# Prompt attention moved block by block into the page stream of a one-core decoder step, and the hand-over of two accumulator banks ahead of the keys-values stage moved up

## What is computed

```python
def diff_attn_prompt(q, k, v, lam):          # query blocks of 128, causal, 4 blocks
        s = jnp.einsum('bqhmd,bkhmd->bhmqk', qi, k) * ATTN_SCALE
        s = jnp.where(kpos[None, :] <= qpos[:, None], s, -jnp.inf)
        p = jax.nn.softmax(s, axis=-1)
        w = p[:, :, 0] - lam * p[:, :, 1]
        return jnp.einsum('bhqk,bkhd->bqhd', w, v)
def diff_attn_sample(q, k_past, v_past, k_new, v_new, lam):   # 8 sequences, 16 pages of 128 past tokens each
    s_past = ...; s_new = ... (causal among the 8 new tokens)
    p = jax.nn.softmax(jnp.concatenate([s_past, s_new], axis=-1), axis=-1)
    w = p[:, :, 0] - lam * p[:, :, 1]
    return einsum(w[..., :P], v_past) + einsum(w[..., P:], v_new)
```

## Time and profile before

| | us |
|---|---|
| median of three runs (lowest, highest) | 2148.5 (2145.39, 2149.3) |
| the profiled execution, its own time | 2154.17 |
| its span, first to last instruction | 2152.3 |
| TensorE busy | 1875.1 (87%) |
| VectorE busy | 838.2 (39%) |
| ScalarE busy | 735.3 (34%) |
| GpSimd busy | 155.8 (7%) |
| moved by DMA | 301.07 MB, mean 140 GB/s |

### The profile page before, as it was taken

The page is one execution under the profiler, slowest core; times in us unless marked ns, Lnnn a source line. Parts: engine busy times, 40 slices in busy tenths (PEclk is TensorE's granted clock), DMA queues, the critical chain, the costliest instruction groups (busy, mean ns, idle before and its releaser), DMA issues.

```text
span 2152.3 us, 43567 instructions
## 1 busy us (share of the span) xinstructions
PE 1875.1 (87%) x17223; PEld 1662.3 (77%) x17223; DVE 838.2 (39%) x1423; ACT 735.3 (34%) x1111; POOL 155.8 (7%) x305
## 2 busy tenths in 40 slices
PE   4997889799999996998757798888866899999998
PEld 2583689799999996998623576767636899999997
DVE  6558223423323333127788422222226433233222
ACT  2423333433333223225433454434312343333222
POOL 2010012100000121001011100000003300000000
PEclk7578999899999998999867899999867899999999
DMA  8748642122222322221200499989880122222222
GB/s 258 253 163 269 220 120 78 53 81 81 81 84 64 87 80 71 60 78 40 95 33 0 141 348 366 380 339 370 328 264 27 52 79 78 88 82 72 81 80 71
DMA packets 245007, 301.07 MB, mean 140 GB/s; under 512 B 10188, under 2 KB 195472, under 8 KB 244816
## 3 DMA queue, kind: packets, MB, share of 16 engines
q1 hardware_dynamic: 241752, 290.22, 40.5%
q10 hardware_dynamic: 2432, 8.16, 1.1%
q0 software_dynamic: 704, 0.95, 0.2%
HBM read 291.92 MB, written 7.37 MB: 139 GB/s over the span
## 4 chain that ended last, share of the span: by engine, by line
PE 68%; DVE 9%; DMA 8%; issue 5%; SPq 5%; ACT 3%; POOL 1%; DVEq 0%; POOLq 0%; ACTq 0%
PE ps L578 53%; PE ps L501 4%; DMA kpg<-in_cache_k 4%; DVE t L1813 2%; SPq L452 2%; PE ps L528 2%; SPq L459 2%; DMA raw<-in_w_ada_mix 1%; DMA vpg<-in_cache_v 1%; PE ps L717 1%; PE ps L952 1%; PE ps L856 1%; DMA raw<-in_w_ada_ffn 1%; DVE l L1893 1%; PE ps L908 1%
## 5 line engine op out<-in xcount | busy, mean ns | idle before, releaser
L578 PE MATMUL ps<-hr,ws 128*128 128x288 f32 x5760 | 783.1, 298 | 48.7 <-ACT rstd L1084 16.2
L578 PEld LDWEIGHTS ps<-hr,ws 128*128 128x128 f32 x5760 | 778.2, 191 | 52.8 <-issue 44.0
L1765 DVE TENSOR_TENSOR ws<-raw,ws 128x1024 fp32r<-128x1024 f32 x200 | 234.9, 1176 | 710.4 <-ACT ws L1210 710.4
L1210 ACT ACTIVATE ws<-raw 128x1024 fp32r<-128x1024 f32 x200 | 201.2, 1008 | 700.5 <-PE ps L578 643.5
L578 PE MATMUL ps<-gr,ws 128*128 128x288 f32 x2112 | 279.4, 294 | 0.0
L578 PEld LDWEIGHTS ps<-gr,ws 128*128 128x128 f32 x2112 | 279.1, 188 | 0.0
L1378 ACT ACTIVATE kTs<-ps 128x512 f32<-128x512 f32 x256 | 139.0, 597 | 177.3 <-PE ps L501 176.7
L501 PE MATMUL ps<-ident,kpg 128*128 128x128 f32 x1024 | 142.8, 285 | 33.1 <-DMA kpg<-in_cache_k 31.6
L501 PEld LDWEIGHTS ps<-ident,kpg 128*128 128x128 f32 x1024 | 115.6, 145 | 60.9 <-ACT kTs L1378 30.4
L528 PE MATMUL ps<-raw,cond 128*32 128x256 f32 x896 | 88.3, 509 | 44.5 <-DMA raw<-in_w_ada_mix 32.6
L578 PE MATMUL ps<-hg,ws 128*128 128x288 f32 x768 | 106.0, 301 | 8.9 <-DVE ws L1765 8.9
(11 more groups left out here) (315 smaller groups left out, 1663.0 us busy)
## 6 DMA issues: line engine op xcount, KB each, us to landing
kpg<-in_cache_k SPq DMA_DIRECT2D x128, 512.0 KB, 5.9
vpg<-in_cache_v SPq DMA_DIRECT2D x128, 512.0 KB, 6.0
raw<-in_ffn_w SPq DMA_DIRECT2D x88, 512.0 KB, 3.7
raw<-in_w_ada_mix SPq DMA_DIRECT2D x48, 512.0 KB, 5.3
raw<-in_w_ada_ffn SPq DMA_DIRECT2D x48, 512.0 KB, 4.7
raw<-in_ffn_w SPq DMA_DIRECT2D x48, 384.0 KB, 3.4
raw<-in_w_ada_kv SPq DMA_DIRECT2D x16, 512.0 KB, 5.4
raw<-in_ssm_w_glu SPq DMA_DIRECT2D x16, 512.0 KB, 4.1
```

The lines of the kernel that those rows point to most:

```text
L578: return mm(ps[:, 4 * s + 2 * tile + h, 0:HALF], ws[:, (u * S + j) % 2, w, k, :], src[:, k0 + k, v, h * HALF:(h + 1) * HALF], start=(k0 + ...
L1210: A(ws[:, w, 0, 0:nk, :].rearrange("p k n -> p (k n)"), raw[:, slot, 0:nk, :].rearrange("p k n -> p (k n)"), ACT.Copy).then_inc(slab_high, 1)
L1765: TT(f(ws[:, w, 1, 0:nk, :]), f(raw[:, slot, 0:nk, :]), f(ws[:, w, 0, 0:nk, :]).bitcast(F32), ALU.subtract).then_inc(raw_done[slot], 1)
```

## The change

Prompt attention has no stage of its own. Turns 2 to 9 of the stream hold the eight heads, one block to each quarter of a turn (block n = 4 x (turn - 2) + quarter). On TensorE the scores of block n come after page 1 of the first quarter and after page 0 of the others; the transposes of block n - 1 come ahead of the values of page 0 of each quarter; the previous head's values come after page 0 of a turn. ScalarE does the block's exps after the quarter's last page, and the head's output after page 1 (behind the sequence's exp); VectorE does `block_turned(n - 1)` and `block_max(n)` ahead of a quarter's copy of turned weights and `block_weights(n)` behind it. The last block and head follow turn 9.

Blocks have one set of buffers now: banks 2 and 3 for scores, bank 2 again for transposes, bank 3 for the head's values; key pages are turned in banks 0 and 1 only, new scores and outputs use the free half of bank 6. `vtok` lies in `raw`, so SyncE waits for the last head's values ahead of the `wo` weights. New values come ahead of new scores at a turn's end. The loops over turns are written out. GpSimd's copies of heads go; VectorE waits for `tri` and for the tokens' writes ahead of the stream.

Ahead of `kv` ScalarE signals `free[1]` right after `root(2)`, by a tiny copy; the copy to `rstd` stays where it was and has a signal of its own, `rstd_kept`, for which `apply("q")` waits on VectorE.

```diff
-    vtok = share("vtok", [P, QB, H, DV], 118 * KB)
-    e01 = share("e01", [P, 2, 2, SEQ], 134 * KB)
+    vtok = raw
+    e01 = share("e01", [P, 2, SEQ], 106 * KB)
...
@@ SyncE @@
                 for b in range(DB, DB + LAG):
                     loads(b, keys=False)
+                sp.wait_ge(pv_full, H)
                 slabs("wo", one)
@@ TensorE @@
-            def block_scores(h, hp, i):
+            def block_scores(n):
+                h, i = n // QB, n % QB
                 w = (i + 1) * P
-                if i == 0:
-                    pe.wait_ge(head_in, h + 1)
-                pe.wait_ge(e_done, h * QB + (i + 1))
+                if n:
+                    pe.wait_ge(wp_copied, n)
+                if i == 0 and h:
+                    pe.wait_ge(head_out, h)
...
-            def block_weights(h, i):
-                pe.wait_ge(w_done, h * QB + (i + 1))
-                pe.wait_ge(wp_copied, h * QB + (i + 1))
+            def block_weights(n):
+                i = n % QB
+                pe.wait_ge(w_done, n + 1)
...
-            def head_values(h, hp):
-                pe.wait_ge(wp_copied, h * QB + (QB + 2))
-                pe.wait_ge(head_out, h + 1)
+            def head_values(h):
+                pe.wait_ge(wp_copied, (h + 1) * QB)
+                if h:
+                    pe.wait_ge(head_out, h)
...
-                    bank = ((par * PAGES + u) * 2 + half) % 3
-                    if not isinstance(at, int) or at > 2:
-                        pe.wait_ge(kt_ready, at - 2)
+                    if at > 1:
+                        pe.wait_ge(kt_ready, at - 1)
...
                     if keys and u < PAGES - 1:
                         turn_page(b, par, u + 1)
+                    n = n0 + u // 4
+                    if u % 4 == 0 and n > 0:
+                        block_weights(n - 1)
                     if vals:
                         values(b, u)
                     if keys:
                         scores(b, par, u)
+                    if vals and u == 0 and n:
+                        head_values(n // QB - 1)
+                    if vals and u % 4 == (u < 2):
+                        block_scores(n)
                     if vals and u % 4 == 2:
                         turn_weights(b, par, u // 4 + 1)
                 if vals:
                     pe.wait_ge(vn_full, 16 * (b - LAG + 1))
                     pe.wait_ge(wt_copied, (b - LAG + 1) * 5 + 1)
+                    new_values(b)
                 if keys:
                     new_scores(b, par)
                 if vals:
-                    new_values(b)
                     outputs(b)
...
+            for b in range(DB + LAG):
+                sequence(b)
+            block_weights(H * QB - 1)
+            head_values(H - 1)
@@ ScalarE @@
             root(2)
+            norm_read(2)
             apply("kv")
-            norm_read(2)
+            A(halves(rstd[:, :]), ps[:, 6:8, 0:HALF], ACT.Copy).then_inc(rstd_kept, 1)
             dense("kv")
...
                 for u in range(PAGES):
+                    if b < DB:
+                        page(b, b, u)
+                    if 0 < b <= DB and u == 1:
+                        weights(b, b)
+                    n = n0 + u // 4
+                    if n > 0 and u == 1:
+                        head_output(n // QB - 1)
+                    if n >= 0 and u % 4 == 3:
+                        block_exp(n)
@@ VectorE @@
                 if vals:
                     weights(b, 0)
-                if soft:
+                if 0 < b <= DB:
                     normalize(b, par)
                 for q in range(4):
+                    n = (b - LAG) * QB + q
+                    if n > 0:
+                        block_turned(n - 1)
+                    if n >= 0:
+                        block_max(n)
                     if vals:
                         weights(b, q + 1)
+                    if n >= 0:
+                        block_weights(n)
                     if keys:
                         scores(b, par, q)
```

More of the change, by code:

```diff
@@ L871, in _ @@
-            for i in range(2):
-                block_scores(0, 0, i)
-            head_pair(0, first=True)
-            with pe.Fori(1, H // 2 - 1) as k:
-                head_pair(k)
-            head_pair(H // 2 - 1, final=True)
-            head_values(H - 1, 1)
-            pe.wait_ge(head_out, H + 1)
             def turn_page(b, par, u):
@@ L888, in turn_page @@
                     at = (b * PAGES + u) * 2 + half
-                    bank = ((par * PAGES + u) * 2 + half) % 3
-                    if not isinstance(at, int) or at > 2:
-                        pe.wait_ge(kt_ready, at - 2)
+                    if at > 1:
+                        pe.wait_ge(kt_ready, at - 1)
                     for h in range(4):
-                        last = turn(ps[:, bank, h * P:(h + 1) * P], kpg[:, slot, 4 * half + h, :])
+                        last = turn(ps[:, half, h * P:(h + 1) * P], kpg[:, slot, 4 * half + h, :])
                     last.then_inc(k_turned, 1)
@@ L1384, in weights, with sequence @@
                 A(q, q, ACT.Exp, bias=mq[:, 1, 0:1], scale=SCALE, accum_out=mq[:, 1, 1:2]).then_inc(e_full, 1)
-            def sequence(b, par, keys=True, soft=True):
+            def sequence(b):
+                n0 = (b - LAG) * QB
                 for u in range(PAGES):
-                    if keys:
-                        page(b, par, u)
-                    if soft and u == 1:
-                        weights(b, par)
-            sequence(0, 0, soft=False)
-            sequence(1, 1)
-            with act.Fori(0, (DB - LAG) // NBUF) as i:
-                for v in range(NBUF):
-                    sequence(i * NBUF + (LAG + v), LAG + v)
-            sequence(DB, DB, keys=False)
+                    if b < DB:
[7 more added lines that the diff above has]
+                        block_exp(n)
+            for b in range(DB + LAG):
+                sequence(b)
+            head_output(H - 1)
+            act.wait_ge(head_out, H)
             act.wait_ge(o_ready, DB + 1)
@@ L1601, in _ @@
                 new_keys(b, b)
+            for s in range(2):
+                pool.wait_ge(tok_put[s], 16 * (6, 4)[s])
             new_values(0)
@@ L2008, in sequence @@
                     outputs(b)
-            sequence(0, 0, vals=False, soft=False)
-            sequence(1, 1, vals=False)
-            with step.loop(0, (DB - LAG) // NBUF, 5 * NBUF) as i:
-                for v in range(NBUF):
-                    sequence(i * NBUF + (LAG + v), LAG + v)
-            sequence(DB, DB, keys=False)
-            sequence(DB + 1, DB + 1, keys=False, soft=False)
+            for b in range(DB + LAG):
+                sequence(b)
+            block_turned(H * QB - 1)
             split(SLABS["wo"] - DENSE0)
```

168 lines of the change are left out of this document (51 added, 117 removed).

## The result

The changed kernel takes 2079.9 us (median of 4 runs, 2070.7 to 2081.5) beside 2148.9 for the kernel before: a ratio of 0.967, interval 0.964 to 0.970. The forecast was 2074, range 2045 to 2105. The profiled execution is one of 2080.7 us with a span of 2078.9, against 2152.3 before.

The account below looks back on a forecast made before the run. It saw an attention stage without transfers, then turns where TensorE waits for pages that SyncE issues late. Terms -120.8 - 12.5 + 38.5 + 10 + 10.6 = -74.2, off the median of 2148.5, gave 2074 us, range 2045 to 2105.

Parts of the forecast that it names:

- Cost 0: Key pages turned in two banks instead of three: no cost, as ScalarE's copies are covered; 7 us if not.
- The stage removed: Prompt attention's own stage goes: first stream scores 122.3 us earlier, +1.5 for a low clock, net -120.8 us.
- The keys-values stage: Its first 96 products start early, beside the making of their input: -12.5 us, between 9 and 13.
- Attention's products: TensorE's prompt-attention work in the six keys-and-values turns: 6.5 us a head, bounds 5.7 and 10.3, +35.5 us in all.
- The stall: At a turn's start the previous head's values wait for VectorE's last weight copy: 3.7 us, five turns, +18.5 us.
- Key-page waits: TensorE's 30.2 us of waits for key pages in six turns: 24 given back as cover, bounds 10 and 30.
- The loop: TensorE's 4.03 us gap where the loop over turns starts over disappears: -4 us.
- The turn's end: New scores now follow new values, so TensorE waits longer for VectorE's output copy: +5 us, 0 to 8.
- Why pages were late: SyncE's loads start 1.23 us apart or more, so 16 key and 16 value pages take some 40 us.
- The last two turns: Turns with values alone: two heads' work partly hidden, with a stall at the first's start, +10 us, bounds 5 and 21.
- The end: Output weights are loaded only after the last head's values, with nothing covering it: +10.6 us, bounds 7 and 13.
- the first rival: Transfers and SyncE keep the turns' pace, so attention only fills waits: 2045 to 2055 us, chance 0.13.

Follow-up runs that it names:

- before_early_bank: Kernel before with only the early signal of free[1] right after the root, the rstd copy with its own signal: 2139.3 us, ratio 0.994.
- before_again: Kernel before, unchanged, run as a kernel of its own: 2151.5 us, ratio 0.9997.
- exp_table: Changed kernel with a tiny exp on ScalarE ahead of the stream, so the exp table is loaded there: 2076.1 us, ratio 0.963.
- all_four: Changed kernel with the edits of copy_first, exp_table, bank7 and wo_early together: 2043.5 us, ratio 0.949.
- best: weights_last, exp_table and wo_early in one kernel: 2039.5 us, ratio 0.948.
- copy_first: Changed kernel with VectorE's copy of the last block's turned weights put ahead of the weight row's scaling at a turn's start: 2050.8 us, ratio 0.953.
- bank7: Changed kernel with new scores in the free part of bank 7 and again ahead of new values: 2078.3 us, ratio 0.967.
- weights_last: copy_first with VectorE's operations on the weights of a turn's last block put behind new scores, bias and output copy: 2043.8 us, ratio 0.951.
- no_attention: Changed kernel with the prompt attention's blocks and heads left out of the stream: 2018.0 us, ratio 0.937.
- before_no_loop: Kernel before with only TensorE's loop over the six turns written out: 2141.2 us, ratio 0.994.
- fixed_pages: no_attention with page addresses computed from SyncE's loop counter instead of read from the page table: 2012.4 us, ratio 0.935.
- wo_early: Changed kernel with the last head's values copied by GpSimd, so output weights load one head earlier, and ScalarE's splits ahead: 2068.7 us, ratio 0.962.

## Why the prediction was right, step by step

The forecast was 6 us too low. The differences in the table, without the 6.0 us ahead of the change, come to -67.5, and the medians differ by 69.0; the forecast was -74.2. The step that the forecast had wrong is what the change costs the stream beside attention: "Cost 0" for two key banks, and no term for the rest. It measured 8 us in the six turns and 4.6 on average in the two before them, and which part of the change it is stays open. Other terms were off both ways, and their sum came near by luck in part.

**The stage removed** was right. GpSimd's memset is followed by the first scores 2.55 us later, as before:

```profile
1066.99 0.10 POOL L1526 MEMSET mark<- 128x1 f32 x1
...
1069.54 1.04 PE L887 MATMUL ps<-kTs,qn 128*32 128x128 f32 x16 [3.10 <-POOL kn L1542]
```

Of the -124.1, 1.9 belong to the early bank (before_early_bank has them too), which leaves -122.2 for -122.3; the +1.5 of a low clock lies in the two turns behind. Without the 6.0 us ahead of the change the first scores would have come at 1075.5, for 1078.

**The keys-values stage** was right, -13.0 for -12.5, with those 1.9 beside: 14.8 by itself in before_early_bank.

**Two turns with keys alone** are where this shows most: "Cost 0 by that cover" for two key banks, and a low clock of +1.5 at most. They cost +7.5. Busy time of the first, after:

```profile
1069.54:1098.20 28.66, 25.14 (x368) 19.21 (x369) 4.13 (x6) 15.32 (x28) 2.50 (x11) 0.94 0.72 243
```

and in before_again:

```profile
1206.60:1233.10 26.50, 23.61 (x368) 18.11 (x369) 4.13 (x6) 15.38 (x29) 2.48 (x11) 1.00 0.86 293
```

TensorE comes out of a 3.1 us wait for GpSimd's new keys and is granted 0.94 in place of 1.00; it is busy 1.5 us longer in this turn, and as much in the next. The rest are waits, over both turns 3.2 for ScalarE's page copies (0.8 before) and 3.5 for pages (1.4). Of the copies' waits 1.4 go with the table load, now in the second turn (exp_table). The 7.5 is not the typical size: the four profiles of kernels with the old stream have 53.0 to 55.2 us for these two turns, the seven with the changed kernel's two turns (exp_table, all_four and best aside) 56.5 to 60.7, on average 4.6 more. Which part two banks cost was not measured alone.

**The six turns** were right in sum, +40.8 for +38.5, but not part by part. Attention's products: 5.7 a head, the lower bound, for 6.5, so 30.7 for 35.5. The stall: 16.7 us in five turns, 3.56 in turn 7, the one worked out, for 18.5 and 3.7. Low clock behind it: 7.9 less busy time in copy_first, 6.2 of it in the head's values, for 7.5; behind two of the five stalls the clock did not fall. Key-page waits in these turns went from 30.2 to 11.2, 19 given back for 24. The loop: 9 for 4. The turn's end: the wait for the output copy rose from 4.3 to 10.9 in six turns, 6.6 for 5, but the reason given was wrong: bank7 undoes the order of new scores and values and leaves the wait, weights_last shortens VectorE's queue and takes 0.7 a turn. With these sizes the sum is 30.7 + 16.7 + 7.9 + 6.6 - 9 - 19 = 33.9, 7 us short of the 40.8. They lie in what the forecast put at nothing: without attention the six turns of the changed kernel still take 277.1 us (no_attention) where those of the kernel before without its loop take 268.8 (before_no_loop), 8.3 more, in single profiles, and a little of it is counted in the turn's end already. So the sum came within 2.3 us by luck: the products and the give-back of the pages were put too high, and the loop and this cost too low.

**Why pages were late**, SyncE's 1.23 us, was wrong, without harm to a number: the loads are about as far apart as a page's transfer takes, 512 KB at 408 GB/s being 1.28 us, and fixed_pages shows that issuing faster does not move more. The forecast had weighed the Trainium skill (DMA: Bandwidth & Descriptors, Specifications) with its 358 GB/s as a core's share. The same page, in its section Bandwidth, gives that figure to a core whose neighbour on the same memory streams too, and has 425 GB/s for a load of 16 MB by a single core. An estimate by that figure is 238 us for the 101 MB; at this case's plateau of 410 they would take 246, and no_attention's six turns last 277, since the rate falls to 251 to 282 at the turns' edges. The trace is near the second figure and above the first.

**The last two turns** were right, +11.1 for +10. Waits for value pages fell from 14.3 to 4.0 us, and TensorE waits 8.0 for blocks' weights and 4.9 for the output copy (1.1 before) in their place.

**The end** was right, +11.2 for +10.6, and wo_early takes 7.3 of it back.

Of the rivals none came: turns 3 to 7 take 52 to 57 us and not 46; a wait of the transposes for a block's weights is not in the list of the six turns; page turning waits for ScalarE 0.3 us in one of them. But copy_first shows that the first rival was nearer than its 0.13 says: with the stall gone, attention costs 28.7 us of TensorE and 16.5 of time. Two of the signs were narrowly missed: key-page waits of 11.2 us, for under 10, and a split 11.8 us behind the last output product, for about 10.

What stays open: what two key banks and the changed orders each cost by themselves, and new scores first together with late weights.

## What to carry to other kernels

When work is woven into a stream, follow each new copy through the queue of its engine: here one copy that needed nothing stood behind a scaling that waited for another engine's exponential, and it cost 29 us of what the move could bring. In a stream that is near its transfers' pace, do not count on shorter page waits to hide a new wait of the consuming engine: the slots that it doesn't free are loads that aren't started. Here 16.7 us of such waits came back as 15.9 us of idle time when they were removed, and 7.9 us of busy time on top, as the clock had fallen behind some of them. When a kernel gets more than one change, compare what is left of the stream without the new work with the old stream: here that showed 8 us that no term had. A pace of issues that equals the pace of transfers says nothing about which of them sets it; make one of them faster to see.

## What the runs showed of the hardware

Loads of 512 KB, each to 128 partitions, move at little over 400 GB/s on this one core (slices of 403 to 418 away from the turns' edges, and mostly 391 to 418) whether they are issued down to 0.6 us apart or 1.25; the median time from issue to landing of a key page grows from 6.0 to 7.7 us instead. After waits of 3.0 to 3.6 us TensorE's 512-wide fp32 products took 941 ns on average, and without the wait 645; behind two of the five waits, 3.55 and 3.56 us long, they were as fast as without. Without the reading of each page's number from memory into SyncE's register, a turn of 46 us with 32 loads was 1.1 us shorter in one profile each, a difference that the kernels' times don't confirm.
